# First half of the output projection for three row blocks, moved into attention heads 1 to 6 and kept in DRAM

## The reference

```python
q, k, v -> per block of 128 rows: index scores, top 256 keys, softmax attention, 8 heads of 64
y_conv = group_rmsnorm(y_conv, gn_conv, CONV_GROUPS) * jax.nn.silu(cz)
y_attn = group_rmsnorm(y_attn, gn_attn, N_HEADS) * jax.nn.silu(az)
y = jnp.concatenate([y_conv, y_attn], axis=-1) @ w_out
out = rmsnorm(x + gate[:, None, :] * y, norm_f)
```

## Time and profile before

| | |
|---|---|
| median of 3 runs | 735.82 us (734.84 to 737.59) |
| the profiled execution, its own time | 735.85 us |
| span of the profile | 734.0 us |
| PE / DVE / ACT / POOL busy | 669.8 / 482.9 / 360.3 / 224.2 us |
| mean granted clock of PE | 0.99 |

### The profile page before, as it was taken

One profiled execution on the slowest core, in us unless ns is written; L12 is line 12 of the kernel. 1 busy time (PEld: TensorE's weight loads), 2 busy tenths in 40 slices (PEclk: granted clock), 3 DMA queues, 4 the chain that ended last, 5 costly groups with the idle time before them and its releaser, 6 DMA issues.

```text
span 734.0 us, 8761 instructions
## 1 busy us (share of the span) xinstructions
PE 669.8 (91%) x3170; PEld 549.3 (75%) x3170; DVE 482.9 (66%) x737; ACT 360.3 (49%) x545; POOL 224.2 (31%) x109
## 2 busy tenths in 40 slices
PE   0479999899999999999999999998999988979996
PEld 0468988678888888878878787786777666758885
DVE  4786816677888899998079420014898988585734
ACT  1484434555563143441443514535787787783212
POOL 0003324432224152747655476510011110030000
PEclk9999999999999999999999999998999999999999
DMA  8902287353332111111100541076744340301431
GB/s 343 412 27 87 65 212 140 115 171 114 89 87 86 58 52 35 57 33 53 58 29 29 202 144 57 1 171 176 226 115 116 87 116 4 113 29 58 171 116 57
DMA packets 22661, 79.14 MB, mean 108 GB/s; under 512 B 3738, under 2 KB 4058, under 8 KB 21596
## 3 DMA queue, kind: packets, MB, share of 16 engines
q1 hardware_dynamic: 22620, 78.60, 35.1%
HBM read 61.77 MB, written 13.41 MB: 102 GB/s over the span
## 4 chain that ended last, share of the span: by engine, by line
PE 77%; DVE 8%; ACT 5%; issue 5%; DMA 3%; SPq 1%; ACTq 0%; DVEq 0%
PE ps L628 17%; PE ps L629 17%; PE ps L630 17%; PE ps L803 4%; PE ps L804 4%; PE ps L805 4%; PE ps L741 3%; PE ps L686 2%; PE ps L687 2%; PE ps L667 2%; PE ps L668 2%; DMA xin<-in_x 2%; DVE phL L1374 2%; DMA wa<-in_w_ada 2%; PE ps L754 1%
## 5 line engine op out<-in xcount | busy, mean ns | idle before, releaser
L628 PE MATMUL ps<-hH,wH 128*128 128x512 f32 (+1 forms) x592 | 231.1, 390 | 2.3 <-issue 1.2
L629 PE MATMUL ps<-hL,wH 128*128 128x512 f32 (+1 forms) x592 | 227.5, 384 | 0.0
L630 PE MATMUL ps<-hH,wL 128*128 128x512 f32 (+1 forms) x592 | 227.3, 384 | 0.0
L1523 POOL TENSOR_TENSOR wL<-raw,wH 128x1024 fp32r<-128x1024 f32 x37 | 94.7, 2559 | 195.8 <-ACT wH L857 195.8
L628 PEld LDWEIGHTS ps<-hH,wH 128*128 128x128 f32 x592 | 111.4, 188 | 25.1 <-issue 6.1
L630 PEld LDWEIGHTS ps<-hH,wL 128*128 128x128 f32 x592 | 111.4, 188 | 21.2
L629 PEld LDWEIGHTS ps<-hL,wH 128*128 128x128 f32 x592 | 111.5, 188 | 19.7 <-issue 1.0
L1366 DVE CUSTOM_DVE_ANT_0 ps<-ps,bias 128x128 f32<-128x128 f32 (+3 forms) x64 | 48.7, 761 | 46.5 <-PE ps L668 44.6
L1374 DVE TENSOR_TENSOR phL<-ps,phH 128x512 fp32r<-128x512 f32 (+1 forms) x96 | 52.7, 555 | 22.7 <-ACT phH L1030 18.7
L1010 ACT ACTIVATE relu<-ps,wabs 128x384 f32<-128x384 f32 (+5 forms) x48 | 40.1, 849 | 43.6 <-PE ps L687 17.7
L1260 DVE SCALAR_TENSOR_TENSOR score<-relu,wsgn,score 128x384 f32<-128x384 f32 (+5 forms) x42 | 49.7, 1183 | 17.2 <-ACT relu L1010 14.5
(11 more groups left out here) (201 smaller groups left out, 1074.7 us busy)
## 6 DMA issues: line engine op xcount, KB each, us to landing
raw<-in_w_units SPq DMA_DIRECT2D x36, 512.0 KB, 3.4
wa<-in_w_ada SPq DMA_DIRECT2D x8, 1024.0 KB, 8.8
ks<-qk_halves SPq DMA_DIRECT2D x32, 256.0 KB, 5.5
xin<-in_x SPq DMA_DIRECT2D x8, 512.0 KB, 12.6
gw<-in_w_ada SPq DMA_DIRECT2D x8, 512.0 KB, 4.4
qs<-qk_halves SPq DMA_DIRECT2D x16, 256.0 KB, 4.0
...
```

The lines of the kernel that those rows point to most:

```text
L628: pe.matmul(out, wH[:, n % 2, kt, :], hH[:, kt, cols], start=(kt == 0), stop=False)
L629: pe.matmul(out, wH[:, n % 2, kt, :], hL[:, kt, cols], start=False, stop=False)
L630: mm = pe.matmul(out, wL[:, n % 2, kt, :], hH[:, kt, cols], start=False, stop=(kt == KT - 1))
L1523: g.tensor_tensor(wL[:, n % 2, :, :], raw[:, n % NRAW, :, :], wH[:, n % 2, :, :].bitcast(F32), ALU.subtract).then_inc(s_wL, 1)
```

## The change

1. **Fills.** In heads 1 to 6, slots 2 to 5, PE does one step each of part 0 for row blocks 4, 5 and 6 (`fill_step`; head h takes block 4 + (h-1)//2, columns half (h-1)%2) into PSUM bank 3. DVE multiplies the bank by the gate at x = 24h + 12 (`fill_gate`), and in heads 2, 4, 6 adds `x` (`fill_add`); SP stores the 128 by 1024 result in DRAM (`store_part`) and loads it later in the place of `x` (`load_x`). Blocks 4 to 6 then need only part 1. The operands are made by `fill_high` (ACT) and `fill_low` (DVE) in the head before.
2. **Weights.** Tiles 0 to 3 are loaded first and all split in head 0 and after it; tiles 4 to 7 are loaded after the last store and split in head 7, ACT and DVE.
3. **Order.** The first `group_sums` of a pair goes from slot 5 to slot 6, the first `pair_add` one slot later; the 16 early steps of head 7 are spread differently; `high` and `low_y` of blocks 1 to 3 come later; `pair_gate(3, 1)` comes before the `pair_scale` calls.
4. Buffers move: `woB`, `yH`, `yL`, `xe`, `oe`, `te`.

```diff
-SUMS_AT = {24 * (2 * t + 2) + 11 + 4 * half: (t, half) for t in range(NT - 1) for half in range(2)}
+SUMS_AT = {24 * (2 * t + 2) + 13 + 2 * half: (t, half) for t in range(NT - 1) for half in range(2)}
...
-ADD_AT = {24 * (2 * t + 2) + 13 + 4 * half: (t, half) for t in range(NT - 1) for half in range(2)}
+ADD_AT = {24 * (2 * t + 2) + 15 + 2 * half: (t, half) for t in range(NT - 1) for half in range(2)}
...
-OUT_HIGH_AT = {24 * (2 + ct) + 15: ct for ct in range(4)}
-EARLY_PARTS = {4: 2, 5: 2, 6: 2, 7: 3, 8: 3, 10: 2, 11: 2}
+OUT_HIGH_AT = {17 + 2 * ct: ct for ct in range(4)}
+OUT_HIGH_AT.update({LAST + 15 + 2 * ct: 4 + ct for ct in range(4)})
+OUT_LOW_AT = {LAST + 17 + 2 * ct: 4 + ct for ct in range(4)}
+EARLY_PARTS = {3: 1, 4: 2, 5: 2, 6: 2, 7: 1, 9: 2, 10: 3, 11: 3}
+
+FILLS = {h: (4 + (h - 1) // 2, (h - 1) % 2) for h in range(1, 7)}
+FILLED = tuple(sorted({b for b, _ in FILLS.values()}))
+FILL_STEPS = (2, 3, 4, 5)
+FILL_BANK = 3
+FILL_GATE_AT = {24 * h + 12: h for h in FILLS}
+FILL_ADD_AT = {24 * h + 13: FILLS[h][0] for h in FILLS if FILLS[h][1]}
+FILL_HIGH_AT = {24 * h - 4: FILLS[h][0] for h in FILLS if FILLS[h][1] == 0}
+FILL_LOW_AT = {24 * h - 2: FILLS[h][0] for h in FILLS if FILLS[h][1] == 0}
...
 # SP
+            def store_part(n):
+                sp.wait_ge(s_f0, n + 1)
+                sp.dma_start(dpart[n], part0[:]).then_inc(s_fst, 16)
+            def load_x(b):
+                src = dpart[FILLED.index(b)] if b in FILLED else a["x"][0, P * b:P * b + P, :]
...
                 if h == 2:
                     sp.wait_ge(s_unit, NU)
+                    for ct in range(NT):
+                        sp.dma_start(wo[:, ct, :], a["w_out"][P * ct:P * ct + P, :]).then_inc(s_wo, 16)
...
                 if h >= 3 and h % 2:
-                    spread_den((h - 3) // 2)
+                    n = (h - 3) // 2
+                    if n:
+                        store_part(n - 1)
+                    sp.dma_start(xf[:], a["x"][0, P * FILLED[n]:P * FILLED[n] + P, :]).then_inc(s_xf, 16)
+                    spread_den(n)
+            store_part(len(FILLED) - 1)
+            sp.wait_ge(s_fst, 16 * len(FILLED))
+            for ct in range(NT, KT):
+                sp.dma_start(wo[:, ct, :], a["w_out"][P * ct:P * ct + P, :]).then_inc(s_wo2, 16)
...
 # PE
+                if h >= 1 and h - 1 in FILLS and i == 4:
+                    pe.wait_ge(s_fm, fill_count(h))
...
                 if t < NT - 1:
                     pe.wait_ge(s_exp, NB * (2 * t + 2) + 7 + half)
+                    pe.wait_ge(s_fm, fill_count(2 * t + 3))
...
+            def fill_step(h, ct):
+                b, half = FILLS[h]
+                n = FILLED.index(b)
+                if ct == 0:
+                    pe.wait_ge(s_fH, n + 1)
+                    pe.wait_ge(s_fL, n + 1)
+                    pe.wait_ge(s_exp, NB * h + 7)
+                if h == 1:
+                    pe.wait_ge(s_woH, ct + 1)
+                    pe.wait_ge(s_woL, ct + 1)
+                out = ps[:, FILL_BANK, :]
+                cols = slice(HALF * half, HALF * half + HALF)
+                pe.matmul(out, yfH[:, ct, :], wo_high(ct)[:, cols], start=(ct == 0), stop=False)
+                pe.matmul(out, yfH[:, ct, :], hL[:, ct, cols], start=False, stop=False)
+                mm = pe.matmul(out, yfL[:, ct, :], wo_high(ct)[:, cols], start=False, stop=(ct == NT - 1))
...
+                if k // STEPS in FILLS and k % STEPS in FILL_STEPS:
+                    fill_step(k // STEPS, FILL_STEPS.index(k % STEPS))
...
             for b in range(4, NB):
-                out_part(b, 0)
+                if b not in FILLED:
+                    out_part(b, 0)
                 out_part(b, 1)
...
 # ACT
-                if k == LAST // 2 + 4:
+                if k == LAST // 2 + 7:
                     high(1, 0)
...
-            for ct in LATE_OUT:
-                out_high(ct)
...
 # DVE
+                v.tensor_tensor(part0[:, cols], ps[:, FILL_BANK, :], gatef[:, cols], ALU.mult).then_inc(s_fm, 1)
+                v.tensor_tensor(part0[:], part0[:], xf[:], ALU.add).then_inc(s_f0, 1)
+                v.tensor_tensor(yfL[:], yconv[:, :, P * b:P * b + P], yfH[:].bitcast(F32), ALU.subtract).then_inc(s_fL, 1)
...
-                if k == LAST // 2 + 5:
+                if k == LAST // 2 + 8:
                     low_y(1, 0)
-                if k == LAST // 2 + 10:
+                if k == LAST // 2 + 11:
                     low_y(2, 0)
-                    low_y(3, 0)
             head_out(2 * NH - 1)
+            low_y(3, 0)
+            pair_gate(NT - 1, 1)
             for t in range(NT - 1):
                 pair_scale(t)
             pair_scale(NT - 1, 0)
-            pair_gate(NT - 1, 1)
-            low_out(5)
             pair_add(NT - 1, 1)
-            low_out(7)
```

More of the change, by code:

```diff
@@ L178 @@
 Y_SLOTS = 4
-Y_ORDER = [(b, 0) for b in range(4)] + [(b, 1) for b in range(4)] + [(b, part) for b in range(4, NB) for part in range(2)]
+Y_ORDER = [(b, 0) for b in range(4)] + [(b, 1) for b in range(4)] + [(b, part) for b in range(4, NB) for part in range(b in FILLED, 2)]
 Y_AT = {y: n for n, y in enumerate(Y_ORDER)}
-LATE_OUT = (4, 5, 6, 7)
-LATE_DVE = (5, 7)
 def build(nc, a):
@@ L574, in _ @@
                     sp.wait_ge(s_res, b + 1)
[L575 removed]
+                    load_x(b + 2)
             for half in range(2):
@@ L779, in out_step @@
                     pe.wait_ge(s_yL, n + 1)
-                if part == 0 and ct == 0:
-                    if b >= 4:
-                        pe.wait_ge(s_og, b - 3)
-                    elif b == 0:
+                first = NT if b in FILLED else 0
+                if b >= 4 and ct == first:
+                    pe.wait_ge(s_og, b - 3)
+                if b < 4 and ct == 0:
+                    if b == 0:
                         pe.wait_ge(s_exp, NB * NH - 1)
@@ L1131, in _ @@
                 if b + 4 < NB:
-                    high(b + 4, 0)
+                    if b + 4 not in FILLED:
+                        high(b + 4, 0)
                     high(b + 4, 1)
@@ L1432, in low_y, with fill_gate, fill_add, fill_low @@
                                 yH[b % Y_SLOTS][:, k, :].bitcast(F32), ALU.subtract).then_inc(s_yL, 1)
+            def fill_gate(h):
+                b, half = FILLS[h]
+                n = FILLED.index(b)
+                dve.wait_ge(s_gf, 16)
+                dve.wait_ge(s_fill, 2 * n + half + 1)
+                if half == 0 and n:
+                    dve.wait_ge(s_fst, 16 * n)
+                cols = slice(HALF * half, HALF * half + HALF)
+                v.tensor_tensor(part0[:, cols], ps[:, FILL_BANK, :], gatef[:, cols], ALU.mult).then_inc(s_fm, 1)
+            def fill_add(b):
+                n = FILLED.index(b)
+                dve.wait_ge(s_fm, 2 * n + 2)
+                dve.wait_ge(s_xf, 16 * (n + 1))
+                v.tensor_tensor(part0[:], part0[:], xf[:], ALU.add).then_inc(s_f0, 1)
+            def fill_low(b):
+                dve.wait_ge(s_fH, FILLED.index(b) + 1)
+                v.tensor_tensor(yfL[:], yconv[:, :, P * b:P * b + P], yfH[:].bitcast(F32), ALU.subtract).then_inc(s_fL, 1)
             for u in range(NB):
@@ L1482, in _ @@
                 if b + 4 < NB:
-                    low_y(b + 4, 0)
+                    if b + 4 not in FILLED:
+                        low_y(b + 4, 0)
                     low_y(b + 4, 1)
```

101 lines of the change are left out of this document (60 added, 41 removed).

## The result

| | before | with the change |
|---|---|---|
| median, 4 runs each | 735.33 us (734.53 to 737.59) | 747.45 us (746.62 to 748.07) |
| ratio, 95% interval | | 1.0158 (1.014 to 1.0176) |
| the profiled execution, its own time | 735.85 us | 748.07 us |
| span | 734.0 us | 746.3 us |
| mean granted clock of PE | 0.99 | 0.98 |

The kernel became 1.6% slower: the forecast had the sign right (slower by 4.2 us), and the size wrong: it is 12.2 us by the profiles and 12.1 by the medians, outside the range of 731 to 745.

The account below looks back on a forecast made before the run. PE's stream bounds the kernel, each head a loop of PE, ACT and DVE. Tail -22.8, head 0 +5.1, head 1 +1.1, heads 3 and 5 +3.2, even heads +11.1, head 7 +6.5: +4.2 on 735.85, so 740.0 us; range 731 to 745.

Parts of the forecast that it names:

- The tail: After attention: 72 fewer matmuls win 16.3 us, the stall 4.9, the slow stretch behind it 1.6; in all 22.8.
- Rival 5: Tail: DVE's epilogue sets blocks 0 to 6 at 6 us or more, 4 us missing, 744 us; chance 0.05.
- the sentence on `fill_gate`: Fills in the heads, on DVE: `fill_gate` waits for the store of the part before, 0 to 1 us, taken as 0.
- Head 7: Last head: block 1's low part comes late for PE, 4.9 us lost (bounds 0 and 6), plus 1.6 for the clock.
- Rival 2: Head 7 does not stall, 733.5 us; with cheaper head 0 or even heads, 732.1 to 739.5; chance 0.37.
- Head 0: First head: ACT's added copies delay head 1's exponentials, 4.1 us lost (bounds 2 and 4.8), plus 1.0 for the clock.
- The port: Head 0: `fill_low` meets POOL's subtracts, up to 2.4 us on DVE, taken as hidden by ACT's delay.
- rival 4: Head 0: `fill_low`, beside POOL's subtracts, is not hidden, +2.4, 742.4 us; chance 0.05.
- Odd heads: Heads 1, 3, 5: PE's fills cost 1.6 us each in heads 3 and 5, 1.1 in head 1.
- Even heads: Heads 2, 4, 6: PE's fills and serial DVE work cost 3.9 us in heads 2 and 4, 3.3 in 6.
- Rival 1: Heads: PE's holes take the fills, each head costs only the lower bound, head 7 0; 724.9 us; chance 0.16.

Follow-up runs that it names:

- experiment 1: The changed kernel with the stores of parts 0 and 1 issued one head earlier, in heads 2 and 4: 739.10 us.
- experiment 4: The changed kernel with fills for blocks 4 and 5 alone (heads 1 to 4), block 6 whole in the tail: 745.01 us.
- experiment 2: The changed kernel with head 7 reordered: block 1's low part before tile 4's split, that split a slot later, first early step in slot 4: 741.02 us.
- experiment 6: The changed kernel with early stores, head 7 reordered, and `fill_add` and blocks 5 and 6's `fill_low` on POOL instead of DVE: 730.28 us.
- experiment 10: The changed kernel with early stores, head 7 reordered and `fill_gate` ahead of `pair_gate`, adds still on DVE: 730.25 us.
- experiment 7: The kernel of experiment 6 with `fill_gate` ahead of `pair_gate` on DVE in heads 2, 4 and 6: 726.82 us.
- experiment 8: The kernel of experiment 1 with the two middle of each fill's four steps left out: 731.86 us, one run.

## Why the prediction was wrong, point by point

**The tail was right.** 22.8 us forecast, 23.1 found. PE has no wait of any kind in the tail of the changed kernel. The epilogue of seven blocks:

```profile
L1581 DVE TENSOR_TENSOR te<-ps,gate x7: 1215/1218/1225, 696.2 to 730.4; 128x1024 f32<-128x1024 f32 x7
```

The times are the first and the last start, so (730.4 - 696.2)/6 = 5.7 us lie from one to the next, at the forecast's own limit, and PE, 61.10 busy of 61.10, does not wait for it; DVE is only about 0.3 us a block behind the pace of PE's 5.44. Rival 5 falls.

**The step that failed** is the sentence on `fill_gate`: "It also waits for the store of the part before; the store is issued about 3 us before it, so 0 to 1 us, taken as 0." The time of issue was placed well (566.89, and the gate could have started at 573.45 - 3.28 = 570.17): only the landing was wrong. "0 to 1 us" leaves it 3 to 4 us, which fits a store with the queue to itself; the six loads in front of it on SP were not counted, though the store's place behind them could be read from the code. The landing took 6.4 us, the gate waited 3.28, PE 2.96 and then ran at 0.60. It came twice. Heads 3 and 5 together are +8.2 us over their forecast where the whole miss is 8.1 by the profiles; experiment 1 gives back 8.3 in the median. None of the prediction's rivals held it.

**Head 7** went as forecast and cost more, 9.2 for 6.5. Block 1's `yL` was forecast ready 641.5 - 618.1 = 23.4 us after the head's start and was ready at 668.82 - 644.1 = 24.7. From there to the last values the forecast had 6.7 us and 1.6 for the clock; it took 9.6, with the clock low for 7 us instead of 3.6. In experiments 1 and 4, where head 7 is the same, the clock stayed at 1.00 behind the slot 3 step's wait of 1.76; there PE goes on 23.2 us after the head's start, as forecast, and the head lasts 32.7 and 32.9. So about 1.5 of the 2.7 us missed are the low clock behind the first wait, which some executions have and some have not, and the rest is the mis-sized clock behind the second. Rival 2, that head 7 would not stall, falls; experiment 2 shows that it would have held had the order been another.

**Head 0** was oversized for this profile: +2.1, for 5.1. The mechanism is there. PE's wait for an exponential, then ACT's first operations of the row that causes it, then DVE's `fill_low`, all of the changed kernel:

```profile
522.34 0.50 PE L709 MATMUL ps<-ks,qs 128*128 128x512 f32 x1 [2.19 <-ACT prob L1036]
```

```profile
517.40 1.05 ACT L1127 ACTIVATE hH<-wo 128x1024 fp32r<-128x1024 f32 x1
518.35 0.48 ACT L1093 ACTIVATE phH<-ps 128x384 fp32r<-128x384 f32 x1
```

```profile
521.81 1.97 DVE L1529 TENSOR_TENSOR yfL<-yconv,yfH 128x512 fp32r<-128x512 f32 x1
```

But ACT's 4.8 us are not 4.8 us on PE: the one long wait is 2.19, and the rest runs beside PE's own work. That the term was too high is in part this execution's luck. Heads 0 and 1 together cost +3.6 here, for a forecast of 6.2; in six of the ten profiles that have these splits and fills they cost +5.5 to +5.7, for a reason told below.

**The port** (rival 4): `fill_low` of head 0 took 1.97 us where the other two took 0.69 and 0.69, so it was slowed by 1.3 us beside POOL's subtracts. The two subtracts that it met:

```profile
520.86 2.37 POOL L1698 TENSOR_TENSOR hL<-wo,hH 128x1024 fp32r<-128x1024 f32 x1
```

```profile
523.20 2.83 POOL L1698 TENSOR_TENSOR hL<-wo,hH 128x1024 fp32r<-128x1024 f32 x1
```

PE has no wait behind it longer than 0.24 in the stretch that follows, so the delay stayed hidden, as the forecast had it. The Trainium skill, SBUF — State Buffer, section Who interferes with whom, has such operations fully block one another; by that rule the operation may lose any part of a subtract, up to its 2.4 us. The 1.3 found lies within it, and 1.97 with 2.90 and 3.37 makes three slow rows, each beside POOL. The rows speak for blocking and against sharing. The first subtract lasted 2.37 us, no more than one alone, though `fill_low` stood beside it for 1.4; `fill_low`, whose rows alone are 0.69 long, ended 0.55 us after it, at 523.78; and the subtract that followed was 0.44 over the median of 2.39. In the kernel before, `pair_gate` (0.74 alone) ended at 653.39, which is again 0.55 us after the end of the subtract that it had met (649.88 + 2.96 = 652.84).

**Odd heads**: 1.6 us forecast for the fills; 1.5 us found in heads 1, 3 and 5 once the store is out of the way. **Even heads**: 3.9 and 3.3 forecast, 3.1 found in each, so the sum of 11.1 was 1.7 too high. Here the size was near and the reason wrong in part. The forecast saw that `group_sums` waits for the gate, but it priced the adds as serial too; experiment 6 takes the adds away for nothing. In the order as built the gate's wait covers them; experiment 10 against 7 shows that they cost 0.7 us once that wait is gone.

**Rival 1** (PE's holes take the fills) falls by the windows, with odd heads at 17.2 for its 16.8 and even ones at 20.3 for its 18.7, and by experiment 8, where an odd head saves 0.7 of 1.36 us. The forecast for odd heads, that 1.1 of 2.72 us fit into holes, stands.

The account closes: +8.2 (heads 3 and 5, the store) + 2.7 (head 7) + 1.5 (the start, scatter) + 0.4 (head 1) - 3.0 (head 0) - 1.7 (even heads) - 0.3 (tail) = 7.8, of the 8.1 between 748.07 and 740.0; 0.2 more lie behind the last matmul, and the rest is rounding. Without the store's wait the time would have been 739.1 (experiment 1), where the forecast said 740.0; that closeness is partly luck, since the errors of head 7, of the start, of the even heads and of head 0 cancel, and some of them differ from one execution to another.
